# Sums of squares for two norms a layer moved from GpSimd to ScalarE and VectorE, statistics one to three pieces later

## The reference

```python
for l in range(2):
    h = rmsnorm(x, norm_mix[l])              # first norm of the layer
    p = h @ w_in[l]                          # 2048 -> 4608: q, k, v (1024 each), pool 512, conv 1024
    y_b = diff_attention(q, k, v, lam, ...)  # 8 heads, two softmax maps each
    y_a = multiscale_pool(p[..., 3072:3584], ...)
    y_c = conformer_conv(p[..., 3584:], ...) # value * sigmoid(gate), 31 taps, LayerNorm, swish, 512x512
    x = x + concat([y_b, y_a, y_c]) @ w_out[l]
    h = rmsnorm(x, norm_ffn[l])              # second norm of the layer
    gu = h @ w_ffn_in[l]                     # 2048 -> 2 x 5504
    g = causal_dwconv(gu[..., :5504], ...)   # 3 taps
    x = x + (silu(g) * gu[..., 5504:]) @ w_ffn_out[l]
return rmsnorm(x, final_norm)                # last norm

def rmsnorm(x, g):
    return x * rsqrt(mean(x * x, axis=-1) + 1e-6) * g
```

## Time and profile before

| | |
|---|---|
| time, median of 3 runs | 2135.47 us (2132.7 to 2137.67) |
| the profiled execution's own time | 2137.0 us |
| its span, first to last instruction | 2135.2 us |
| TensorE, matmuls | 2095.3 us busy, 98% of the span |
| VectorE | 1462.4 us, 68% |
| ScalarE | 1073.1 us, 50% |
| GpSimd | 155.0 us, 7% |
| mean granted TensorE clock | 0.996 |

### The profile page before, as it was taken

The page is one execution under the profiler, slowest core; times in us unless marked ns, Lnnn a source line. Parts: engine busy times, 40 slices in busy tenths (PEclk is TensorE's granted clock), DMA queues, the critical chain, the costliest instruction groups (busy, mean ns, idle before and its releaser), DMA issues.

```text
span 2135.2 us, 35664 instructions
## 1 busy us (share of the span) xinstructions
PE 2095.3 (98%) x11874; PEld 1818.4 (85%) x11874; DVE 1462.4 (68%) x2049; ACT 1073.1 (50%) x1504; POOL 155.0 (7%) x158
## 2 busy tenths in 40 slices
PE   7999999999999999999999999999999999999997
PEld 6878888888888888888888788888888888888886
DVE  7897777667666665554479977777666676655555
ACT  5447644555555554443363575455455554544433
POOL 4001122000000000110000001310000000001110
PEclk9999999999999999999999999999999999999999
DMA  7544355565555655556655444565555656555553
GB/s 253 176 161 154 128 194 186 181 199 191 187 186 184 199 187 189 190 176 195 196 203 182 151 148 158 175 200 189 192 190 177 199 187 192 188 189 192 190 189 137
DMA packets 108530, 391.77 MB, mean 183 GB/s; under 512 B 12176, under 2 KB 12688, under 8 KB 108176
## 3 DMA queue, kind: packets, MB, share of 16 engines
q1 hardware_dynamic: 107136, 386.98, 55.3%
q10 hardware_dynamic: 1296, 3.55, 0.5%
HBM read 388.38 MB, written 2.10 MB: 183 GB/s over the span
## 4 chain that ended last, share of the span: by engine, by line
PE 85%; DVE 7%; issue 5%; POOL 1%; ACT 1%; DVEq 0%; DMA 0%; SPq 0%; ACTq 0%; POOLq 0%
PE bank L1094 53%; PE bank L1095 27%; DVE gt L713 3%; DVE wlo L664 2%; PE bank L1163 2%; PE bank L1152 1%; PE bank L1154 1%; PE bank L1153 1%; POOL ssq L1033 0%; POOL sq L1030 0%; ACT whi L371 0%; DVE qT L670 0%; DMA x<-xT 0%; DVE E L761 0%; DVE x L1015 0%
## 5 line engine op out<-in xcount | busy, mean ns | idle before, releaser
L664 DVE TENSOR_TENSOR wlo<-raw,whi 128x1024 fp32r<-128x1024 f32 x728 | 912.0, 1260 | 613.0 <-ACT whi L371 612.1
L1094 PE MATMUL bank<-xg,whi 128*128 128x512 f32 x3648 | 1281.6, 396 | 21.1 <-DVE wlo L653 8.3
L371 ACT ACTIVATE whi<-raw 128x1024 fp32r<-128x1024 f32 x728 | 763.6, 1056 | 747.9 <-PE bank L1095 704.3
L1095 PE MATMUL bank<-xg,wlo 128*128 128x256 f32 x3648 | 1020.9, 280 | 0.0
L1094 PEld LDWEIGHTS bank<-xg,whi 128*128 128x128 f32 x3648 | 687.2, 188 | 182.3 <-issue 13.4
L1095 PEld LDWEIGHTS bank<-xg,wlo 128*128 128x128 f32 x3648 | 691.3, 190 | 0.2
L1094 PE MATMUL bank<-hidden,whi 128*128 128x512 f32 x1376 | 486.0, 396 | 0.3
L1095 PE MATMUL bank<-hidden,wlo 128*128 128x256 f32 x1376 | 388.1, 282 | 0.0
L1094 PEld LDWEIGHTS bank<-hidden,whi 128*128 128x128 f32 x1376 | 258.7, 188 | 63.5 <-DVE wlo L664 1.6
L1095 PEld LDWEIGHTS bank<-hidden,wlo 128*128 128x128 f32 x1376 | 258.6, 188 | 0.0
L1094 PE MATMUL bank<-mix,whi 128*128 128x512 f32 x512 | 182.3, 398 | 0.4 <-DVE mix L839 0.4
(11 more groups left out here) (137 smaller groups left out, 1004.8 us busy)
## 6 DMA issues: line engine op xcount, KB each, us to landing
raw<-wstream SPq DMA_DIRECT2D x729, 512.0 KB, 3.4
pw_sb<-pww ACTq DMA_DIRECT2D x2, 1024.0 KB, 5.5
x<-xT SPq DMA_DIRECT2D x3, 512.0 KB, 8.7
outT<-x SPq DMA_DIRECT2D x6, 256.0 KB, 2.1
x<-xT SPq DMA_DIRECT2D x2, 256.0 KB, 4.2
raw<-wstream SPq DMA_DIRECT2D x2, 256.0 KB, 4.0
poolw_sb<-poolw ACTq DMA_DIRECT2D x2, 256.0 KB, 3.4
outT<-x SPq DMA_DIRECT2D x1, 512.0 KB, 3.0
```

The lines of the kernel that those rows point to most:

```text
L371: nc.scalar.activation(whi[:, s, :], raw[:, s, :], ACT.Copy).then_inc(hi_ready, 1)
L664: nc.vector.tensor_tensor(wlo[:, s, :], raw[:, s, :], whi[:, s, :], ALU.subtract).then_inc(lo_ready, 1)
L1094: nc.tensor.matmul(ps[bank][:], whi[:, s, blk * P:blk * P + P], mov, start=first, stop=False)
L1095: return nc.tensor.matmul(ps[bank][:, 0:S], wlo[:, s, blk * P:blk * P + P], mov[:, 0:S], start=False, stop=last)
```

## The change

The sums of squares of both norms of a layer are made in quarters of four chunks. ScalarE squares a quarter in one instruction of 128x1024 into a buffer that is free at that time (y, gt, half of qT, half of kT); VectorE adds quarters 1 to 3 to quarter 0, and folds the four chunks of the sum into `ssq` in two more adds. GpSimd's sums and ScalarE's four single squares at a layer's start go. The squares stand behind pieces 5, 6, 7 and 7, the adds behind 6, 7 and 8, the folds behind 9; `stats(0)` moves from piece 5 to 8, `rms(0)` and `inverse_rms(0)` from 8 to 11. `evac_c(CV)` no longer waits for rstd: its tiles are evacuated unscaled, and `scale_conv_values` multiplies them behind piece 13. In the second norm the squares stand behind B0+11, B0+19, B0+27 and C0+3, the adds each one piece later, the folds behind C0+4; `stats(1)` moves from C0+5 to C0+6, its Sqrt and reciprocal from C0+8 to C0+9. The last norm keeps its `square_sum` on GpSimd, now behind the loop.

```diff
+        quarter_of = [y[:], gt[:, :, 0:S], qT[:, 0:4, :], kT[:, 0:4, :]]
...
+                def square_quarter(n, q):
+                    if n:
+                        act.wait_ge(evacuated, l * TILES + TB + 4 * q + 4 + CREDIT)
+                    nc.scalar.activation(quarter_of[q], x[:, 4 * q:4 * q + 4, :], ACT.Square).then_inc(quarter_squared, 1)
...
-                at(8, rms, 0)
+                for q, (idx, late) in enumerate(((5, B0 + 11), (6, B0 + 19), (7, B0 + 27), (7, C0 + 3))):
+                    at(idx, square_quarter, 0, q)
+                    at(late, square_quarter, 1, q)
+                at(11, rms, 0)
...
-                at(C0 + 8, rms, 1)
+                at(C0 + 9, rms, 1)
...
-                for i in range(NT):
-                    act.wait_ge(evacuated, l * TILES + CREDIT - 3 + i)
-                    square(i)
                 run(4, 5)
...
                         step(nc.vector.memset(glu[:, :, 0:PAD], 0.0))
-                        dve.wait_ge(rstd_ready, l * 2 + 1)
                     add_halves(TA[g], A_BANKS[g], dst, H0[g])
-                    if g == CV:
-                        step(nc.vector.tensor_tensor(glu[:, :, PAD:], glu[:, :, PAD:], rbc(NT), ALU.mult))
-                    else:
+                    if g == CG:
                         nc.vector.tensor_tensor(half[:], half[:], rbc(NT), ALU.mult).then_inc(gate_scaled, 1)
+
+                def scale_conv_values():
+                    step(nc.vector.tensor_tensor(glu[:, :, PAD:], glu[:, :, PAD:], rbc(NT), ALU.mult))
+
+                def add_quarter(n, q):
+                    dve.wait_ge(quarter_squared, l * 8 + 4 * n + q + 1)
+                    if q > 1:
+                        dve.wait_ge(quarters_added, l * 8 + 4 * n + q - 1)
+                    nc.vector.tensor_tensor(y[:], y[:], quarter_of[q], ALU.add).then_inc(quarters_added, 1)
+
+                def fold_quarters(n):
+                    dve.wait_ge(quarters_added, l * 8 + 4 * n + 3)
+                    nc.vector.tensor_tensor(y[:, 0:2, :], y[:, 0:2, :], y[:, 2:4, :], ALU.add).then_inc(quarters_added, 1)
+                    dve.wait_ge(quarters_added, l * 8 + 4 * n + 4)
+                    nc.vector.tensor_tensor(ssq[:], y[:, 0, :], y[:, 1, :], ALU.add).then_inc(ssq_ready, 1)
...
-                at(8, inverse_rms, 0)
+                for q, (idx, late) in zip((1, 2, 3), ((6, B0 + 20), (7, B0 + 28), (8, C0 + 4))):
+                    at(idx, add_quarter, 0, q)
+                    at(late, add_quarter, 1, q)
+                at(9, fold_quarters, 0)
+                at(C0 + 4, fold_quarters, 1)
+                at(11, inverse_rms, 0)
+                at(13, scale_conv_values)
...
-                at(C0 + 8, inverse_rms, 1)
+                at(C0 + 9, inverse_rms, 1)
...
-            square_sum(12, ssq_part, wait_load)
...
-                square_sum(KC, ssq_ready, lambda c: pool.wait_ge(evacuated, l * TILES + TB + c + 1 + CREDIT))
-                pool.wait_ge(ssq_ready, l * 2 + 2)
-
-                pool.wait_ge(stat_done, l * 2 + 2)
-                square_sum(12, ssq_part, lambda c: pool.wait_ge(evacuated, l * TILES + TD + c + 1 + CREDIT))
                 SEEN["pool"] = st.n
 
+            pool.wait_ge(stat_done, 2 * LAYERS)
+            square_sum(12, ssq_part, lambda c: pool.wait_ge(evacuated, (LAYERS - 1) * TILES + TD + c + 1 + CREDIT))
...
-                at(5, stats, 0)
+                at(8, stats, 0)
...
-                at(C0 + 5, stats, 1)
+                at(C0 + 6, stats, 1)
```

More of the change, by code:

```diff
@@ L116, in lam_init @@
     return 0.8 - 0.6 * math.exp(-0.3 * l)
-STEPS = {"dve": 231, "loop": 5, "pool": 59}
+STEPS = {"dve": 231, "loop": 5, "pool": 5}
 SEEN = {}
@@ L200, in program @@
         ssq_part = sem("ssq_part")
+        quarter_squared = sem("quarter_squared")
+        quarters_added = sem("quarters_added")
         end_squared = sem("end_squared")
@@ L619, in _ @@
                                  scale=1.0 / DM).then_inc(rms_ready, 1)
-            act.wait_ge(ssq_part, LAYERS + 1)
+            act.wait_ge(ssq_part, 1)
             act.wait_ge(xg_ready, 32 * LAYERS + POOL_CHUNKS)
@@ L1036, in square_sum @@
                         nc.gpsimd.tensor_tensor(ssq[:], ssq[:], sq[:, c % 2, :], ALU.add).then_inc(done, 1)
-            def wait_load(c):
-                if c in X_LOADS:
-                    pool.wait_ge(x_loaded[X_LOADS[c]], 16)
-            square_sum(12, ssq_part, wait_load)
             pool.wait_ge(consts_loaded, 16)
@@ L1046, in _ @@
                 st.rebase(l * POOL_STEPS + START)
[L1049 to L1055, removed]
                 pool.wait_ge(conv_done, l * NT + NT)
@@ L1320, in _ @@
                               if u == 0 else None, rel0=D0 + DP * u, hook=False)
-            pe.wait_ge(ssq_part, LAYERS + 1)
+            pe.wait_ge(ssq_part, 1)
             pe.wait_ge(evacuated, LAYERS * TILES - NT + CREDIT)
@@ L1325, in _ @@
             for i in range(NT):
-                pe.wait_ge(end_squared, 4 * LAYERS + i + 1)
+                pe.wait_ge(end_squared, i + 1)
                 last = mm(ps[0][:, 0:S], ones, y[:, i, :], False, i == NT - 1)
```

## The result

The kernel with the change takes **2146.84 us** (median of 5 runs, 2137.82 to 2147.22), the kernel before beside it 2136.53: a ratio of 1.0038, with a 95% interval of 1.0027 to 1.0049. It is slower by 0.4%, where I had forecast 2128.7.

What follows compares the result with a forecast made beforehand. TensorE, busy 98% of the span, was taken as the bound, so only its waits and low clock pay. 7.5 (start) + 0.2 (down projection) - 0.2 (FFN norms) = 7.5 us gave 2128.7 us, range 2125.5 to 2133.

Steps and rivals of the forecast that it cites:

- the norms of the FFN: Second norm, both layers: rstd ready 0.3 us before C0+8, costing 0.1 us a layer, between nothing and 0.8.
- The fifth rival: rstd late at C0+8 in both layers by 1 us or more: gain 5 to 5.5, 2130.3 us; 4 in 100.
- The start, 7.5 us: First layer's start: piece 9 begins at 37.2 instead of 44.73, 7.5 us earlier.
- The stall at piece 8: First layer's start: TensorE waits about 0.7 us for bank 0's evacuation, between nothing and 2.5.
- The first term: First layer's start: a quicker first `wlo` half lets TensorE start earlier, counted as 0.25 us, bounds 0 and 0.5.
- The table load rival: ScalarE's squares draw a 1.28 us table load ahead of piece 6: gain 6.2, 2129.9 us; 3 in 100.
- the rule: Skill's advice to batch activations by table set, a switch costing 2.66 us; one ahead of quarter 0 would leave 4.8 us.
- GpSimd as the cause of VectorE's slowness: First layer's start: beside GpSimd `wlo` takes 1798 ns and `gain_lo` 888; with GpSimd silent 1225 and 480.
- the third rival: Transfers, not GpSimd, slow VectorE at the start; `wlo` stay at 1.8 us, 2138.3 us, slower; 4 in 100.
- The second layer's start: No statistics stall there now, first tile done before piece 7 ends: nothing gained, at most 0.8 us lost.
- The down projection: Layer 0: GpSimd's 12 squares go, and a `wlo` beside them costs 0.57 us too much; 0.2 us gained.

Runs made afterwards that it cites:

- e2: Kernel before with only the second norm's statistics, Sqrt and reciprocal one piece later; GpSimd keeps all its sums: 2155.36 us, ratio 1.0073.
- e3: Kernel before with one line more: TensorE also waits for the second norm's rstd ahead of C0+7, no work moved: 2155.59 us, ratio 1.0086.
- e1: Kernel after with only the second norm's statistics back behind C0+5, its Sqrt and reciprocal back behind C0+8: 2126.2 us, ratio 0.995.
- e4: Kernel after with the second norm's late statistics in bank 7, TensorE waiting for rstd only ahead of group C0+8's fourth tile: 2126.9 us, ratio 0.9958.
- e6: Kernel after with the second norm's late statistics in bank 5, TensorE waiting for rstd only ahead of group C0+8's second tile: 2126.34 us, ratio 0.9962.
- e9: e1 with the first evacuation ahead of the folds and the last norm's GpSimd sum moved to ScalarE and VectorE: 2123.62 us, ratio 0.9944 against kernel before.

## Why the prediction was wrong

**The step that failed** is the term for the norms of the FFN, "0.1 us a layer, between nothing and 0.8". Its timing was right: 0.3 us to spare was forecast and 0.3 measured, and TensorE did not stall. But I priced a wait only by the idle time it causes. The runs showed in its place 8.7 us a layer: a wait that comes through 0.3 us ahead of its matmul leaves the next 1312 pairs at 353.3 ns instead of 346.7, one layer of the 2137.82 us execution by its profile, both layers of the 2146.53 one, and by their times (2145.66 to 2147.47) both layers in the other seven. The fifth rival, "rstd late at C0+8", named the place, at 1 us a layer or more and 4 in 100, but again as a stall. e2 and e3 bring the slow pace into the kernel before, e1, e4 and e6 take it out of the kernel after.

The sum closes with it. 2146.84 less two slow stages is 2146.84 - 17.4 = 2129.4, against 2128.7 forecast. From there the 3.0 us of layer 0's quicker down projection lead to 2126.4, and e1 took 2126.2. That it closes to 0.2 us is in part luck: a half-clock stretch more or less in an execution is 1.7 us, and the 1.0 us above isn't traced.

**The start, 7.5 us: right, and right in its terms but the first.** Piece 4 at 21.77 (21.7 forecast), no wait at pieces 4 to 6, the folds done at 32.7 (32.8), the first tile at 33.4 (33.4). The stall at piece 8 is 0.6 us with its restart (0.7): it begins at 33.40, where 21.77 + 4 x 2.77 = 32.85 was free. Statistics in 0.80 us (0.79), piece 9 at 37.12 (37.2), 7.6 us earlier. The first term, 0.25 us for an earlier start, came out (0.2 with the stalls taken off) by luck. TensorE began at 8.23 in place of 8.33, not 0.5 us earlier; but its pairs took the full pace from 11.60 on in place of 13.62, three slow pairs fewer or 0.9 us; and it then waited 0.46 us at 16.12 for piece 2's `wlo`, which wasn't forecast:

```profile
16.12 0.49 PE L1104 MATMUL bank<-xg,whi 128*128 128x512 f32 x1 [0.46 <-DVE wlo L672]
```

One more detail was off and cost nothing. ScalarE took piece 4 at 17.88, not 17.3, since the weights landed only then:

```profile
17.88 1.06 ACT L374 ACTIVATE whi<-raw 128x1024 fp32r<-128x1024 f32 x1 [0.59 <-DMA raw<-wstream]
...
21.39 1.05 ACT L405 ACTIVATE y<-x 128x1024 f32<-128x1024 f32 x1
...
35.36 1.28 ACT L399 ACT_TABLE_LOAD   x1
```

**The table load rival fell.** The rows above show it: no load stands ahead of the squares; there is one of 1.28 us ahead of Sqrt, as before, and 26 loads in the whole profile before and after. The Trainium skill, "ScalarE: Activation LUTs", section "What ACT_TABLE_LOAD costs", gives some 1283 ns for the load, with which the row agrees, and a drain with it to make 2.66 us; squares that draw no load escape the rule. The drain doesn't show: around the load ahead of piece 2's `whi`, the instruction before ends at 12.36 and the one behind starts at 13.68, 1.32 us in all.

```profile
11.07 1.29 ACT L332 ACTIVATE xg<-x,par 128x256 fp32r<-128x256 f32 x3
12.38 1.28 ACT L374 ACT_TABLE_LOAD   x1
13.68 2.01 ACT L374 ACTIVATE whi<-raw 128x1024 fp32r<-128x1024 f32 x2
```

**GpSimd as the cause of VectorE's slowness: right.** With GpSimd silent, `wlo` takes 1221 ns and `gain_lo` 477, as at the earlier trace rows, and the transfers were no slower meanwhile: 332 GB/s from 13.6 to 22 and 261 from 22 to 30.7, against 317 and 144 before; the third rival, under which they would have stayed at 1.8 us, falls.

**The second layer's start: right.** TensorE has no wait for `wlo`, the statistics or the first evacuation there, before or after.

**The down projection: right in sign, too small.** I took 0.2 us for layer 0; from first to last pair it took 242.7 us in place of 243.4, so 0.6 (the kernel before has two pairs of long steps there, the kernel after none). The 3.0 us of the changed pace were not in it, and the kernel after doesn't get them (455 matmuls in its window), only e1 and e4 to e9.

**What stays open.** What in the chip holds the pace. In the stages C and D of these profiles the pace changes only where TensorE's even stream is broken (at the wait; at the statistics matmul, in e1 from 353 ns in C0 to C0+4 to 347 behind it; at a long step in the down projection), and lasts for hundreds of microseconds without a wait in sight; whether it comes from the queue, from how weight loads and matmuls interleave, or from instruction fetch, no run here separates. The Trainium skill, "TensorE: Matmul & The Clock Gate", section "Back-to-back issue gap", says that the spacing in a stream of weight loads and matmuls is set by both together, through the window of instructions that TensorE looks at; two paces for one stream would fit that, but the runs don't show the mechanism. Nor is the least lead known, or whether it is the lead and not the distance from the statistics in blocks: 0.3 us gave the slow pace nearly always, 1.0 us in no one of e6's five runs. The third pace, 348.9 ns in the down projection, was only observed. Behind a slow stage C the down projection began at 353.3 in all 7 cases of these profiles; behind a quick one it began at 348.9 in 15 of 17. The two exceptions, layer 0 of the kernels before and after, aren't explained.

## What to carry to other kernels

When you move a wait, don't price it by idle time alone: see how long before the next matmul it comes through. Here 1.0 us was enough and 0.3 was not; putting the awaited bank later in the group bought the difference without moving any other work. When a stage without idle time and at full clock takes longer, count the matmuls in equal windows of both kernels: a difference of 2% in the step is invisible in the chain and in the waits, and over the 1312 pairs of one stage it outweighed here every stall behind the start. And when the executions of one kernel fall into groups a fixed amount apart (2138 and 2147 here), profile one of each before explaining either.

## What the runs showed of the hardware

- TensorE has several steady paces for one stream of pairs (512 and 256 columns, each with its weight load) at a granted clock of 1.00 and without idle time: 346.7, 348.9 and 353.3 ns a pair. A pace lasted for a whole stage of some 460 us.
- Which one it is can differ from execution to execution of one program, and one extra wait instruction moved it in every timed execution of e3.
- While GpSimd worked, VectorE's `wlo` took 1798 ns against 1221, and `gain_lo` 888 against 477. ScalarE's squares of 128x1024 took 1.05 us with VectorE and the transfers running.
